# Wide operations in the second scan's mixing, key norms and end, and the third output stage in blocks of 256 tokens

## The reference

```python
rw = concat([_seq_shift_mix(rw[:, :n_ctx], mu[0], mu[1]),      # z + mu0*(prev-z) + mu1*(next-z)
             _grid_shift_mix(rw[:, n_ctx:], mu)])              # four neighbours in the 64 wide grid
r, k, v, wd_f, wd_b, ad_f, ad_b, gd_r = _split(rw, ...)        # 1152 channels = 9 tiles of 128
kk = k * rwkv_kk
kk = kk / max(sqrt(sum(kk * kk, -1)), 1e-12)                   # per head of 64
y = unboth(_rwkv7_scan(...))                                   # forward and backward
y = ((y - mean(y)) * rsqrt(var(y) + 64e-5)) * rwkv_lnx_w + rwkv_lnx_b
bonus = sum(r * (k_f + k_b) * rwkv_rk, -1) * v
y_rwkv = (y + bonus) * (sigmoid(gd_r) @ rwkv_g2)

x = _layernorm(DN_ALPHA * x + g1 * (y_mix @ w_out), ln1_w, ln1_b)
h = _layernorm(x) * (1 + sc2) + sh2                            # input of the experts
```

## Time and profile before

| | us |
|---|---|
| median of three runs | 5034.46 |
| profiled execution | 5029.4 |
| its span | 5027.5 |
| TensorE busy | 4272.3 (85%) |
| VectorE busy | 2029.2 (40%) |
| ScalarE busy | 1317.2 (26%) |

### The profile page before, as it was taken

How to read it: one execution, slowest core, us unless ns; L and a number is a source line. 1 busy time by engine, 2 the same in 40 slices (tenths; PEclk the granted TensorE clock), 3 DMA queues, 4 the chain that set the end, 5 groups by cost and what they waited for, 6 DMA issues and landing times. The chain is left out here.

```text
span 5027.5 us, 68043 instructions
## 1 busy us (share of the span) xinstructions
PE 4272.3 (85%) x27622; PEld 2396.0 (48%) x27622; DVE 2029.2 (40%) x4149; ACT 1317.2 (26%) x3031; POOL 521.3 (10%) x564
## 2 busy tenths in 40 slices
PE   5998799999997999999987725888588699999991
PEld 2454456644444665454556514777235344334440
DVE  1631556513615664321017576666345222222223
ACT  2111545511115553111124433333021111111111
POOL 0000000000000000000000001222001322322220
PEclk9999889999997999999988857889797899999995
DMA  4011000120110003311110030000303488999983
GB/s 185 21 62 66 6 14 14 69 87 28 62 50 22 10 18 147 134 50 65 67 66 1 2 97 2 3 3 3 109 0 138 167 263 288 323 319 333 336 268 122
DMA packets 148350, 505.31 MB, mean 101 GB/s; under 512 B 22609, under 2 KB 71362, under 8 KB 134594
## 3 DMA queue, kind: packets, MB, share of 16 engines
q1 hardware_dynamic: 110738, 379.89, 20.3%
q0 software_dynamic: 37296, 120.99, 8.7%
HBM read 402.42 MB, written 98.42 MB: 100 GB/s over the span
## 5 line engine op out<-in xcount | busy, mean ns | idle before, releaser
L697 PE MATMUL banks<-arena 128*128 128x512 f32 (+1 forms) x2928 | 1108.4, 540 | 16.4 <-DMA arena<-in_w_in 10.7
L697 PEld LDWEIGHTS banks<-arena 128*128 128x128 f32 x2928 | 559.4, 191 | 564.2 <-issue 522.9
L3111 PE MATMUL banks<-arena 128*32 128x512 f32 (+2 forms) x2896 | 561.4, 595 | 4.2 <-DMA arena<-in_experts 3.3
L884 PE MATMUL banks<-arena 128*128 128x512 f32 (+1 forms) x896 | 377.3, 576 | 24.7 <-DMA arena<-y_d 17.9
L1248 PE MATMUL banks<-arena 96*128 96x512 f32 (+1 forms) x800 | 373.2, 549 | 13.0 <-ACT arena L1351 11.2
L3111 PEld LDWEIGHTS banks<-arena 128*32 128x32 f32 (+2 forms) x2896 | 198.5, 130 | 358.1 <-issue 354.3
L1298 DVE TENSOR_REDUCE arena<-banks 128x1 f32<-128x512 f32 (+1 forms) x400 | 238.3, 596 | 237.7 <-PE banks L1248 236.2
L3130 PE MATMUL banks<-arena 128*32 128x512 f32 (+2 forms) x1448 | 286.4, 595 | 1.7 <-DVE arena L3160 1.2
L884 PEld LDWEIGHTS banks<-arena 128*128 128x128 f32 x896 | 174.4, 196 | 221.1 <-issue 214.9
L3078 POOL DMA_INDIRECT r_d<-arena x125 | 181.4, 1451 | 639.1 <-DVE arena L3160 526.4
L1256 PEld LDWEIGHTS banks<-arena 128*128 128x128 f32 x1312 | 171.2, 143 | 152.8 <-issue 122.0
(11 more groups left out here) (507 smaller groups left out, 5682.1 us busy)
## 6 DMA issues: line engine op xcount, KB each, us to landing
arena<-in_experts SPq DMA_DIRECT2D x64, 3072.0 KB, 13.1
...
arena<-in_w_in SPq DMA_DIRECT2D x19, 1024.0 KB, 5.6
...
arena<-in_w_mod SPq DMA_DIRECT2D x8, 1024.0 KB, 5.2
...
```

The source lines that it names most:

```text
L697: i = e.matmul(self.out_of(n), lhs, rhs, start=k == 0, stop=k == KT - 1)
L884: i = e.matmul(bank(n % 4)[:, 0:nn], w[:, q, :], H[:, q, t0:t0 + nn], start=q == 0, stop=q == KT - 1)
L3111: op = e.matmul(ABK[(q - q0) % 2][rows, :], xT[(q - q0) % 2][:, P * k:P * k + P][:, rows], weights[:, i % SLOTS, 512 * k:512 * k + 512], s ...
```

## The change

In the mixing stage the first three sources are issued ahead of the weights and all nine have a buffer of their own. The order of the sources is k, then the low rank ones, then r and v. ScalarE does the two scalings (`own`), three sources ahead. The context and grid operations alternate, with one wait for two. The key norms are done in this stage in three operations over all ten tiles (40 heads of 64), ScalarE squaring, and the clearings stand ahead of the first source. The scan starts right behind the gate.

At the end four tiles of 256 columns go through each operation at once, in two halves, with the squares on ScalarE, gate products in two banks for each half, and one store of 256 KB for each half and group of 128 channels.

The third output stage takes four blocks of 256 tokens. First norms start at steps 1, 9, 17 and 25, second norms at 14, 22, 30 and 38.

```diff
@@ -2040,27 +2040,37 @@
-        inr, outr = [al(1280), al(1280)], [al(1280), al(1280)]
+        inr, outr = [al(1280) for _ in range(9)], [al(1280) for _ in range(3)]
+        sq, norms = al(2560), al(40)
+        sources = [2, 3, 6, 7, 8, 0, 1, 4, 5]
+        turned = [i for i in sources if i < 6]
+        mixed = lambda i: outr[turned.index(i) % 3] if i < 6 else lo_[i - 6]
+        heads = lambda a: a.rearrange("p (g n) -> p g n", n=64)
...
         def mix_sync(e):
+            def source(i):
+                ld.turn(e)
+                e.dma_start(inr[i], B["rw_d"][P * i:P * i + P, :]).then_inc(ld.hit(mix, "in", i), 16)
+
+            for i in sources[0:3]:
+                source(i)
...
+            for i in sources[3:]:
+                source(i)
...
-            for i in range(9):
-                if i >= 2:
-                    e.wait_ge(*Vn.at("mix", i - 2))
-                ld.turn(e)
-                e.dma_start(inr[i % 2], B["rw_d"][P * i:P * i + P, :]).then_inc(ld.hit(mix, "in", i), 16)
...
         def mix_vector(e):
...
-            e.tensor_tensor(cc_[:, 9:18], cc_[:, 9:18], mu(3), ALU.subtract).then_inc(Vn.hit(), 1)
-            e.wait_ge(*Vn.own())
-            for i in range(9):
-                a, o_ = inr[i % 2], outr[i % 2] if i < 6 else lo_[i - 6]
+            e.tensor_tensor(cc_[:, 9:18], cc_[:, 9:18], mu(3), ALU.subtract).then_inc(Vn.hit("own"), 1)
+            e.memset(BS, 0.0).then_inc(Vn.hit(), 1)
+            e.memset(Y, 0.0).then_inc(Vn.hit(), 1)
+            for n, i in enumerate(sources):
+                a, o_ = inr[i], mixed(i)
                 mc = [reg(cols["mu"] + 9 * j + i, 1) for j in range(4)]
                 og, ag = (v[:, NCTX:T].rearrange("p (r c) -> p r c", c=GRIDW) for v in (o_, a))
-                e.wait_ge(*ld.at(mix, "in", i))
-                if 2 <= i < 6:
-                    e.wait_ge(*Tn.at("turned", i - 2))
-                e.tensor_scalar(o_[:, 0:NCTX], a[:, 0:NCTX], cc_[:, i:i + 1], None, ALU.mult).then_inc(Vn.hit(), 1)
-                e.tensor_scalar(o_[:, NCTX:T], a[:, NCTX:T], cc_[:, 9 + i:10 + i], None, ALU.mult).then_inc(Vn.hit(), 1)
-                e.wait_ge(*Vn.own())
+                e.wait_ge(*Sn.at("own", i))
                 e.scalar_tensor_tensor(o_[:, 1:NCTX], a[:, 0:NCTX - 1], mc[0], o_[:, 1:NCTX], ALU.mult, ALU.add).then_inc(Vn.hit(), 1)
+                e.scalar_tensor_tensor(og[:, :, 1:GRIDW], ag[:, :, 0:GRIDW - 1], mc[0], og[:, :, 1:GRIDW], ALU.mult, ALU.add).then_inc(Vn.hit(), 1)
                 e.wait_ge(*Vn.own())
                 e.scalar_tensor_tensor(o_[:, 0:NCTX - 1], a[:, 1:NCTX], mc[1], o_[:, 0:NCTX - 1], ALU.mult, ALU.add).then_inc(Vn.hit(), 1)
-                e.wait_ge(*Vn.own())
-                e.scalar_tensor_tensor(og[:, :, 1:GRIDW], ag[:, :, 0:GRIDW - 1], mc[0], og[:, :, 1:GRIDW], ALU.mult, ALU.add).then_inc(Vn.hit(), 1)
-                e.wait_ge(*Vn.own())
                 e.scalar_tensor_tensor(og[:, :, 0:GRIDW - 1], ag[:, :, 1:GRIDW], mc[1], og[:, :, 0:GRIDW - 1], ALU.mult, ALU.add).then_inc(Vn.hit(), 1)
                 e.wait_ge(*Vn.own())
                 e.scalar_tensor_tensor(o_[:, NCTX + GRIDW:T], a[:, NCTX:T - GRIDW], mc[2], o_[:, NCTX + GRIDW:T], ALU.mult, ALU.add).then_inc(Vn.hit(), 1)
                 e.wait_ge(*Vn.own())
                 e.scalar_tensor_tensor(o_[:, NCTX:T - GRIDW], a[:, NCTX + GRIDW:T], mc[3], o_[:, NCTX:T - GRIDW], ALU.mult, ALU.add).then_inc(Vn.hit("mix", i), 1)
+                if n == 5:
+                    e.wait_ge(*ld.at(mix, "row", 4))
+                    e.wait_ge(*Sn.at("rows", 5))
+                    e.tensor_tensor(KK, K, rb[4].unsqueeze(1).broadcast_to([P, NT, 256]), ALU.mult).then_inc(Vn.hit("kk"), 1)
+                if n == 7:
+                    e.wait_ge(*Sn.at("sq"))
+                    e.tensor_reduce(norms, heads(sq), AX.X, ALU.add).then_inc(Vn.hit("sum"), 1)
+            e.wait_ge(*Sn.at("root"))
+            e.tensor_scalar(norms, norms, 1e-12, None, ALU.max).then_inc(Vn.hit(), 1)
+            e.wait_ge(*Vn.own())
+            e.reciprocal(norms, norms).then_inc(Vn.hit(), 1)
+            kkh = KK.rearrange("p j n -> p (j n)")
+            e.wait_ge(*Vn.own())
+            e.tensor_tensor(heads(kkh), heads(kkh), norms.unsqueeze(2).broadcast_to([P, 40, 64]), ALU.mult).then_inc(Vn.hit(), 1)
...
         def mix_tensor(e):
-            for i in range(6):
+            for n, i in enumerate(turned):
                 e.wait_ge(*Vn.at("mix", i))
...
+
+            def own(i):
+                a, o_ = inr[i], mixed(i)
+                e.wait_ge(*ld.at(mix, "in", i))
+                if i < 6 and turned.index(i) >= 3:
+                    e.wait_ge(*Tn.at("turned", turned[turned.index(i) - 3]))
+                e.activation(o_[:, 0:NCTX], a[:, 0:NCTX], ACT.Copy, scale=cc_[:, i:i + 1]).then_inc(Sn.hit(), 1)
+                e.activation(o_[:, NCTX:T], a[:, NCTX:T], ACT.Copy, scale=cc_[:, 9 + i:10 + i]).then_inc(Sn.hit("own", i), 1)
+
+            e.wait_ge(*Vn.at("own"))
+            for i in sources[0:3]:
+                own(i)
+            for n, i in enumerate(sources):
+                if i < 6:
+                    dst, c0 = (R, K, V)[i // 2], P * (i % 2)
+                    for q, (t0, w_) in enumerate(groups4):
+                        u = 3 * turned.index(i) + q
+                        e.wait_ge(*Tn.at("rows", u))
+                        e.activation(dst[:, t0:t0 + w_, c0:c0 + P], bank(6 + u % 2)[:, 0:P * w_].rearrange("p (j n) -> p j n", j=w_), ACT.Copy).then_inc(Sn.hit("rows", u), 1)
+                else:
+                    e.wait_ge(*Vn.at("mix", i))
+                    if i != 7:
+                        e.activation(lo_[i - 6], lo_[i - 6], ACT.Tanh if i == 6 else ACT.Sigmoid).then_inc(Sn.hit(), 1)
+                if n + 3 < 9:
+                    own(sources[n + 3])
+                if n == 6:
+                    e.wait_ge(*Vn.at("kk"))
+                    e.activation(sq, KK.rearrange("p j n -> p (j n)"), ACT.Square).then_inc(Sn.hit("sq"), 1)
+                if n == 7:
+                    e.wait_ge(*Vn.at("sum"))
+                    e.activation(norms, norms, ACT.Sqrt).then_inc(Sn.hit("root"), 1)
...
         al.o = mark
-        st_ = al(16)
-        t1, t2, t3 = al(256), al(256), al(256)
...
-        def keys_vector(e):
...
-            e.memset(BS, 0.0).then_inc(Vn.hit(), 1)
-            e.memset(Y, 0.0).then_inc(Vn.hit("zero"), 1)
...
-        keys_vector(dve), keys_scalar(act)
@@ -2527,92 +2537,96 @@
...
-        def begin(e):
-            e.wait_ge(*VC.of("rwkv_keys").at("zero"))
-        begin(pe), begin(act), begin(pool), begin(dve), clear(dve)
+        clear(dve)
...
+        al.o = mark
+        t1, t2, sq = ([al(1024), al(1024)] for _ in range(3))
+        ybuf = [al(1024), al(1024)]
+        mean, root = [al(16), al(16)], [al(16), al(16)]
+        gates = [ps[:, 0:1024], ps[:, 1024:2048]]
+        columns = [ps[:, 2048:3072], ps[:, 3072:4096]]
+        flat = lambda a: a.rearrange("p j n -> p (j n)")
+        each = lambda a: a.unsqueeze(2).broadcast_to([P, 16, 64])
+        row4 = lambda a: a.unsqueeze(1).broadcast_to([P, 4, 256])
+        by4 = lambda a: a.rearrange("p (j n) -> p j n", j=4)
         end = "rwkv_end"
...
         def end_vector(e):
...
+            for i in range(2):
+                y = heads(flat(Y[:, 4 * i:4 * i + 4, :]))
+                e.tensor_reduce(mean[i], y, AX.X, ALU.add).then_inc(Vn.hit(), 1)
+                e.wait_ge(*Vn.own())
+                e.tensor_scalar(mean[i], mean[i], 1.0 / 64, None, ALU.mult).then_inc(Vn.hit(), 1)
+                e.wait_ge(*Vn.own())
+                e.tensor_tensor(heads(t1[i]), y, each(mean[i]), ALU.subtract).then_inc(Vn.hit("sub", i), 1)
+            for i in range(2):
+                v, bonus = heads(flat(V[:, 4 * i + 2:4 * i + 6, :])), BS[:, 16 * i + 8:16 * i + 24]
+                e.wait_ge(*Sn.at("sq", i))
+                e.tensor_reduce(root[i], heads(sq[i]), AX.X, ALU.add).then_inc(Vn.hit(), 1)
+                e.wait_ge(*Vn.own())
+                e.tensor_scalar(root[i], root[i], 1.0 / 64, 64e-5, ALU.mult, ALU.add).then_inc(Vn.hit("var", i), 1)
+                e.tensor_tensor(heads(t2[i]), v, each(bonus), ALU.mult).then_inc(Vn.hit(), 1)
+                e.wait_ge(*Vn.own())
+                e.tensor_tensor(by4(t2[i]), by4(t2[i]), row4(rb[8]), ALU.add).then_inc(Vn.hit(), 1)
+                e.wait_ge(*Sn.at("root", i))
+                e.reciprocal(root[i], root[i]).then_inc(Vn.hit(), 1)
+                e.wait_ge(*Vn.own())
+                e.tensor_tensor(heads(t1[i]), heads(t1[i]), each(root[i]), ALU.mult).then_inc(Vn.hit(), 1)
+                e.wait_ge(*Vn.own())
+                e.tensor_tensor(by4(t1[i]), by4(t1[i]), row4(rb[7]), ALU.mult).then_inc(Vn.hit(), 1)
+                e.wait_ge(*Vn.own())
+                e.tensor_tensor(t1[i], t1[i], t2[i], ALU.add).then_inc(Vn.hit(), 1)
+                e.wait_ge(*Tn.at("gate", i))
```

(42 more changed lines are left out.)

89 lines of the change are left out of this document (5 added, 84 removed).

## The result

The changed kernel takes 4957.4 us, the median of four runs (4944.2 to 4966.7), and the kernel before 5033.3 (four runs, 5031.5 to 5040.2): a ratio of 0.9842, 95% interval 0.9826 to 0.9859. That is 75.9 us less, where 70.2 were forecast; as a time the forecast was 4965, within 4950 to 4988. The profiled execution took 4966.7 (span 4964.8) and was the slowest of the four.

A forecast was written before the change was run, and what follows sets the result against it. Stages run one after the other between gates, mostly bound by VectorE's chain, the output stage by TensorE and its tail. Savings 39.8 + 20.7 + 9.7 = 70.2 from the 5034.5 median gave 4964.3, rounded to 4965 us, range 4950 to 4988.

The forecast's parts named there:

- Mixing, the start: Mixing stage: with three sources issued ahead of the small loads, VectorE starts at 2948.0, 7.7 us earlier.
- The sources: Mixing stage: scalings on ScalarE and two fewer VectorE waits cut each source from 7.09 to 5.82 us, nine to 52.4.
- rival A: Mixing stage: ScalarE's scaling falls behind the turned copies, 10.3 us per source, 93 for nine; 5004 us; chance 0.05 with D.
- The key norms: Mixing stage: wide product and sum take 2.9 us each; 3.6 follow the ninth source; mixing and keys save 39.8.
- just fits: Key norms: ScalarE's square ends at +5.2 us, needed at +5.8; a table load more would cost 0.7.
- Rival D: Scan's start waits for something else, such as the late w2 and a2 loads; 4995 to 5005 us; chance 0.05 with A.
- The scan's end: End stage in two halves of 1024 wide operations takes 30.9 us instead of 51.6, saving 20.7.
- The output stage: Third output stage in 256 wide blocks: start saves 2.5 us, full part loses 19.4, tail saves 26.6; together 9.7.
- The separate +1.4 for halving the instructions: Output stage's full part: twice as many half-width matmuls cost 0.003 to 0.004 us more per pair, over 384 pairs.
- Rival B: Output stage: chained norms cross in the tail, so the quarter blocks bring nothing; 4974 us; chance 0.07.
- Rival C: Output stage: halved matmuls no longer cover weight loads; slower from 0.307 us per instruction, 5110 us at worst; chance 0.02.
- What follows the output stage is gated and starts in the same state: Code behind the third output stage: the prediction claimed it keeps its time, so it adds nothing to the 70.2 us.

The follow-up runs named there:

- sources_last: The changed kernel with SP issuing the twelve small loads of the mixing stage first, then the nine sources; 4954.0 us.
- one_ahead: The changed kernel with ScalarE scaling one source ahead instead of three in the mixing stage; 4970.3 us.
- quarters_only: The kernel before with only the third output stage changed, to blocks of 256; 5023.9 us, ratio 0.9970.

## Why the prediction was right

- **Mixing, the start** (7.7 earlier): 7.5. `sources_last` shows that the place in SP's queue does it.
- **The sources** (5.82 each): 5.79. `one_ahead` shows the condition that rival A named, and its 10.3 for a source that stands behind a turned one; for all nine rival A was too dear (93 against 82.2).
- **The key norms** (2.9, 2.9 and 3.6): 2.82, 2.81 and 3.5. The square "just fits", with 0.5 to spare. Together 40.4 for 39.8. Rival D fell: VectorE's last product ends at 3022.07 and TensorE's first scan instruction starts at 3022.14.
- **The scan's end** (20.7): 22.9. VectorE took 23.3 from its first reduction to its last product (forecast 23.7). The term that was mis-sized is the store: 2.8 for the 4.2 from the copy to the gate. The 3.9 before held more than a store: 1.55 of it passed until GpSimd issued, 0.29 now. Transposes and copies took 2.7 for 3.0.
- **The output stage** (2.5 - 19.4 + 26.6 = 9.7): 2.7, -20.3 and 28.4, together 10.8. In the tail 1.5 of the 1.8 is one term: the last sums of squares were put at 5.3, with a loss to the lower clock as before, and took 3.8 (3715.77 to 3719.53). The separate +1.4 for halving the instructions is too large (two of 0.216 are 0.0026 over 0.4294, 1.0 for 384 pairs), but the sum doesn't use it. Rival B (nothing gained) fell: `quarters_only` gains 10.4 by its stage.
- **Rival C** (weight loads not covered): at 256 columns an instruction takes 0.216, as read. Even at 128 columns load and matmul together take 0.112, so its 0.307 was out of reach.
- **"What follows the output stage is gated and starts in the same state"** is the step that failed: a gate fixes the work but not TensorE's clock. The router's stretch alone is 13 us longer or shorter with nothing changed (35.1 and 22.1), more than the output stage's whole gain. That the forecast was hardly hurt by it is luck in part: before and after were both profiled with the long stretch, and by the medians the untouched rest evened out to 1.8 (75.9 against the stages' 74.1).
